# Prompt latent attention of a two-layer trunk: heads taken in pairs, both heads of a query block behind each other

## The chip, the cores and the metric

The kernel runs on one core of one Trainium2 chip. The metric is the device time of one execution in microseconds (us). TensorE is called PE, VectorE DVE, ScalarE ACT, SyncE SP and GpSimd POOL. All matrix products of the stage that changes are in 32-bit floats; each of them shows in the trace as two matmul records.

## What is computed

Two layers of a hybrid decoder trunk run over 1,024 prompt tokens and 8 x 4 sample tokens. The even layer has multi-head latent attention (8 heads), a linear recurrence and memory attention; the odd layer has an mLSTM, a chunk MLP and memory attention. The change lies in the prompt's latent attention of the even layer:

```
def _mla_scores(q_lat, q_rope, lat, krope):
    s = jnp.einsum('bhqc,bkc->bhqk', q_lat, lat) + jnp.einsum('bhqr,bkr->bhqk', q_rope, krope)
    return s.astype(jnp.float32) * MLA_SCALE
...
    def one_block(args):
        ql, qr, i = args
        s = _mla_scores(ql, qr, latent, k_rope)
        qpos = i * ATTN_BLOCK + jnp.arange(ATTN_BLOCK)
        s = jnp.where(kpos[None, :] <= qpos[:, None], s, -jnp.inf)
        p = jax.nn.softmax(s, axis=-1).astype(latent.dtype)
        return jnp.einsum('bhqk,bkc->bhqc', p, latent)
```

A head's query and key have 64 columns of their own (`NOPE`) and 32 rotated ones (`ROPE`); the key's rotated part is one for all heads. A value has 64 columns. Both kernels project the latent to keys and values of each head first, and so work with 96-row queries and keys.

## The kernel before

The engines run their own programs and wait on semaphores; nothing is scheduled by a tool, so the order in the code is the order on each engine.

**Stages around the change.** The even layer's input projection ends near 290 us of the trace. Then come the memory's keys and values, the convolution and the recurrence (LRU) on DVE and ACT up to 392 us. Its buffers `lru_r`, `lru_i`, `lru_t` lie where attention keeps `kT`, `vh`, `wh`, `probs`, so SP loads the heads' weights `wh` only after `lru_done` (L1960).

**Pieces.** A head is prepared in seven pieces (`piece(h, j)`, L2347 to L2360; evacuated by ACT at L2121 to L2129): two for the key (64 rows x 512), three for the query (96 rows x 352), one for the value of all 8 key blocks, one small one for the sample tokens (`w_ukT`). All pieces use PSUM bank 7, so each waits for the evacuation of the one before (`prep_ev`). DVE then rotates the query's 32 rope rows (`rope(h, step)`, L2270 to L2278). Heads 0 and 1 are prepared ahead of attention (14 pieces); heads 2 to 7 inside it, one piece in each unit (`prep_at`, called as `between(n)`).

**Units.** A unit is one head and one block of 128 queries: `UNITS` has 8 heads x 8 blocks, in a head in the order 7, 0, 6, 1, 5, 2, 4, 3, so a block with 1,024 keys is followed by one with 128, and so on. In one turn n of the loop

- PE does the scores of unit n+1 (L803, bank pair 0/1 or 2/3), the piece, the transposes of unit n (L815, banks 4 and 5) and the output of unit n-1 (L827, bank 6, 64 of the 128 partitions);
- DVE normalises unit n (L882, L884), takes mask and maxima of unit n+1 (L874 to L876), multiplies the output of n-1 into `mx` (L891), and does a rope step;
- ACT evacuates the piece, then the transposed probabilities of unit n (L857), then takes the exponentials of unit n+1 (L846).

`probs`, `probsT` and the score banks have two buffers each. After the last unit come memory attention with the sample group's memory attention between (`pe_blocks`), and the sample group's latent attention.

## Time and profile before

| | |
|---|---|
| median of 3 runs | 1883.89 us (1882.79 to 1888.71) |
| the profiled execution | 1891.48 us, its span 1889.8 us |
| PE busy / weight loads busy | 1618.9 us (86%) / 1380.4 us (73%) |
| DVE / ACT busy | 861.1 us (46%) / 537.1 us (28%) |
| granted TensorE clock, mean | 0.916 of full |
| attention stage (first scores to last output) | 436.2 to 727.0 us |

Times of rows are counted from the start of the span. The granted clock of a stretch is 1.00 at full rate (2.4 GHz) and 0.50 at the lower one (1.2 GHz); a number between is a stretch with both. A busy time in a window counts overlapping records once.

### The profile page before, as it was taken

What the parts mean: (1) busy time and instruction counts of PE and PEld (TensorE: products, weight loads), DVE (VectorE), ACT (ScalarE), POOL (GpSimd) and SP (SyncE); (2) the same over time, 40 slices, a digit from 0 to 9 for tenths busy, and PEclk for the clock granted to TensorE, in tenths of its full rate; (3) what the DMA queues carried; (4) which work ended last, traced back from release to release, by engine and by line L of the source; (5) the groups of instructions that cost most, each with busy time, mean ns of one, the idle gap of its engine ahead of it and who ended that gap; (6) DMA issues with size and microseconds to landing.
All of it is one profiled execution on the core that took longest, in us unless ns stands there. A gap on an engine that the chain in (4) does not pass through costs nothing.

```text
span 1889.8 us, 24206 instructions
## 1 busy us (share of the span) xinstructions
PE 1618.9 (86%) x9962; PEld 1380.4 (73%) x9962; DVE 861.1 (46%) x1525; ACT 537.1 (28%) x993; POOL 33.7 (2%) x61
## 2 busy tenths in 40 slices
PE   6999894358999986698998899989999957886994
PEld 6999892225666654455998899987999935874993
DVE  3222625554655565455486322272222224546574
ACT  2003210603333334344254311110002134322343
POOL 1000000000000000000000100000000010000000
PEclk9999997679999998899998899996999987975997
DMA  4111103010100013254552311110111041003561
GB/s 153 53 49 45 34 12 123 26 33 7 57 1 1 1 45 101 62 156 125 181 172 90 143 46 45 45 34 24 45 45 46 12 168 46 1 6 116 174 204 69
DMA packets 51263, 132.12 MB, mean 70 GB/s; under 512 B 6841, under 2 KB 30570, under 8 KB 49938
## 3 DMA queue, kind: packets, MB, share of 16 engines
q1 hardware_dynamic: 46914, 113.12, 18.8%
q0 software_dynamic: 4240, 17.45, 2.5%
q8 instruction: 80, 1.31, 0.3%
q14 instruction: 29, 0.24, 0.0%
HBM read 117.08 MB, written 13.47 MB: 69 GB/s over the span
## 4 chain that ended last, share of the span: by engine, by line
PE 45%; DVE 7%; issue 3%; ACT 2%; DMA 1%; POOL 0%; DVEq 0%; SPq 0%; ACTq 0%; POOLq 0%
PE ps L499 7%; PE ps L500 7%; PE ps L501 7%; PE ps L558 4%; PE ps L560 3%; PE ps L559 3%; PE ps L1269 1%; PE ps L1044 1%; PE ps L1684 1%; PE ps L1898 1%; PE ps L1294 1%; PE ps L949 1%; PE ps L936 1%; PE ps L1550 1%; PE ps L1552 1%
## 5 line engine op out<-in xcount | busy, mean ns | idle before, releaser
L499 PE MATMUL ps<-x_hi,w_hi 128*128 128x352 f32 x1416 | 463.6, 327 | 30.6 <-DVE w_lo L458 28.2
L500 PE MATMUL ps<-x_lo,w_hi 128*128 128x352 f32 x1416 | 459.1, 324 | 0.0
L501 PE MATMUL ps<-x_hi,w_lo 128*128 128x352 f32 x1416 | 458.7, 324 | 0.0
L499 PEld LDWEIGHTS ps<-x_hi,w_hi 128*128 128x128 f32 x1416 | 270.1, 191 | 32.1 <-DVE w_lo L458 29.0
L500 PEld LDWEIGHTS ps<-x_lo,w_hi 128*128 128x128 f32 x1416 | 270.4, 191 | 0.3
L501 PEld LDWEIGHTS ps<-x_hi,w_lo 128*128 128x128 f32 x1416 | 269.7, 190 | 0.0
L452 ACT ACTIVATE w_hi<-w_raw 128x1024 fp32r<-128x1024 f32 (+1 forms) x107 | 123.1, 1152 | 441.3 <-PE ps L501 322.3
L558 PE MATMUL ps<-mx_hi,w_hi 128*128 128x352 f32 x480 | 159.0, 331 | 14.8 <-issue 13.4
L458 DVE TENSOR_TENSOR w_lo<-w_raw,w_hi 128x1024 fp32r<-128x1024 f32 (+1 forms) x107 | 144.1, 1347 | 60.0 <-ACT w_hi L452 59.5
L560 PE MATMUL ps<-mx_hi,w_lo 128*128 128x352 f32 x480 | 155.4, 324 | 0.0
L559 PE MATMUL ps<-mx_lo,w_hi 128*128 128x352 f32 x480 | 155.2, 323 | 0.0
L479 DVE COPY z<-ps 128x352 f32<-128x352 f32 x90 | 46.8, 524 | 219.5 <-PE ps L501 219.5
L558 PEld LDWEIGHTS ps<-mx_hi,w_hi 128*128 128x128 f32 x480 | 91.2, 190 | 16.4 <-issue 13.4
L481 DVE TENSOR_TENSOR mx<-sig,ps 128x352 f32<-128x352 f32 x60 | 30.9, 520 | 155.8 <-ACT sig L467 155.8
L467 ACT ACTIVATE sig<-ps 128x352 f32<-128x352 f32 x72 | 33.3, 465 | 225.3 <-PE ps L501 225.3
L559 PEld LDWEIGHTS ps<-mx_lo,w_hi 128*128 128x128 f32 x480 | 91.6, 191 | 0.8
L560 PEld LDWEIGHTS ps<-mx_hi,w_lo 128*128 128x128 f32 x480 | 91.2, 190 | 0.0
L803 PE MATMUL ps<-kT,qT 96*128 96x512 f32 (+2 forms) x192 | 82.6, 542 | 0.0
L827 PE MATMUL ps<-probsT,vh 128*64 128x128 f32 x576 | 78.3, 282 | 0.5 <-DVE mx L891 0.5
L2347 PE MATMUL ps<-z,wh 128*64 128x512 f32 x64 | 35.5, 683 | 48.0 <-DMA wh<-in_w_mla 46.2
L827 PEld LDWEIGHTS ps<-probsT,vh 128*64 128x64 f32 x576 | 62.5, 139 | 11.6 <-issue 10.5
L815 PEld LDWEIGHTS ps<-ident,probs 128*128 128x128 f32 x288 | 33.4, 144 | 46.7 <-DVE probs L884 36.0
(413 smaller groups left out, 2033.9 us busy)
## 6 DMA issues: line engine op xcount, KB each, us to landing
w_raw<-in_w_out SPq DMA_DIRECT2D x48, 640.0 KB, 3.9
w_raw<-in_w_in SPq DMA_DIRECT2D x59, 512.0 KB, 3.6
page<-in_cache_mla SPq DMA_DIRECT2D x128, 144.0 KB, 2.7
kvs<-in_mem_cache SPq DMA_DIRECT2D x16, 512.0 KB, 9.2
x_res<-in_xT SPq DMA_DIRECT2D x24, 176.0 KB, 2.3
x<-x_next POOLq DMA_DIRECT2D x1, 4224.0 KB, 13.8
x_res<-x SPq DMA_DIRECT2D x24, 176.0 KB, 2.4
out_y<-res POOLq DMA_DIRECT2D x3, 1408.0 KB, 5.9
```

The costliest lines, as they stand in the source:

```text
L452: act.activation(w_hi[:, u % 2, 0:n], w_raw[:, u % 2, 0:n], ACT.Copy).then_inc(w_hi_ready, 1)
L458: dve.tensor_tensor(w_lo[:, u % 2, 0:n], w_raw[:, u % 2, 0:n], w_hi[:, u % 2, 0:n], ALU.subtract).then_inc(w_split, 1)
L479: ins = dve.tensor_copy(out, zz[0:8] if tile.one else zz)
L499: pe.matmul(out, w_hi[:, u % 2, kk], x_hi[:, k, chunk(c)], start=(k == 0), stop=False)
L500: pe.matmul(out, w_hi[:, u % 2, kk], x_lo[:, k, chunk(c)], start=False, stop=False)
L501: mm = pe.matmul(out, w_lo[:, u % 2, kk], x_hi[:, k, chunk(c)], start=False, stop=(k == KX - 1))
L558: pe.matmul(out, w_hi[:, u % 2, kk], mx_hi[:, k, chunk(c)], start=(k == 0), stop=False)
L559: pe.matmul(out, w_hi[:, u % 2, kk], mx_lo[:, k, chunk(c)], start=False, stop=False)
L560: mm = pe.matmul(out, w_lo[:, u % 2, kk], mx_hi[:, k, chunk(c)], start=False, stop=(k == KM - 1))
L803: mm = pe.matmul(s[:, a:b], q_of(u), k_of(u, a, b), start=True, stop=True)
L827: mm = pe.matmul(ps[r:r + 64, 6, 0:P], v_of(u, kt), probsT[:, n % 2, kt, :], start=(kt == 0), stop=(kt == nk - 1))
L2347: mm = pe.matmul(ps[0:64, 7, :], wh[:, s, 288 + 64 * k:352 + 64 * k], z[:, Z_KV + k, 512 * j:512 * j + 512], start=(k == 0), stop=(k == 1))
```

## The change

Heads are handled in pairs. One piece makes the 64 query (or key, or value) columns of two heads at once, 128 columns wide; the 32 rope columns of four heads are one piece of their own (`wr`, `rq`). There are now 42 pieces (9 for each of four pairs, 2 x 3 for the rope) where there were 56. The odd head of a pair keeps its 64 columns in partitions 64 to 127 and the rope rows in 0 to 31, with 32 zero rows between (128 rows); the even head stays as it was (96 rows). The first 12 pieces use eight banks in turn. Six of them stand ahead of the wait on `lru_done` on ACT; their weights lie in the free weight buffer `w_raw` and are loaded before `lru_done`. The other 30 run inside attention, at units 0 to 11, 18 to 26 and 34 to 42.

Units are ordered by pair, block, head: both heads of block 7, both of block 0, both of 6, both of 1 and so on. The output of the two heads is one loop that alternates between the upper and the lower 64 partitions of bank 6, followed by one multiplication over 128 partitions. `probsT` has four buffers.

```diff
...
-        ALTERNATE = [q for a in range(NT // 2) for q in (NT - 1 - a, a)]
-        UNITS = [Unit(h, q, (q + 1) * P) for h in range(H) for q in ALTERNATE]
+        UNITS = [Unit(2 * p + r, q, (q + 1) * P, 8 * p + 2 * a + w)
+                 for p in range(H // 2) for a in range(NT // 2) for w, q in enumerate((NT - 1 - a, a))
+                 for r in range(2)]
+        Pair = namedtuple("Pair", "p q nk first second")
+        PAIRS = [Pair(u.h // 2, u.q, u.nk // P, n, n + 1) for n, u in enumerate(UNITS) if n % 2 == 0]
...
+        def pair_at(n):
+
+            return n // 2 - 1 if n % 2 == 0 and n else None
...
+        ROPE_PIECE = (0, 21)
+        PAIR_PIECE = (3, 12, 24, 33)
+        N_FIRST, N_PIECES = 12, 42
...
+        def piece_bank(i):
+            return i % 8 if i < N_FIRST else 7
...
+            def output(m):
+                w = PAIRS[m]
+                pe.wait_ge(pt_ev, FILLS[w.second][1])
+                pe.wait_ge(prep_ev, PAIR_PIECE[w.p] + 7)
+                if m:
+                    pe.wait_ge(o_done, m)
+                for kt in range(w.nk):
+                    for r, n in enumerate((w.first, w.second)):
+                        mm = pe.matmul(ps[64 * r:64 * r + 64, 6, 0:P],
+                                       vh[:, w.p % 2, kt, 64 * r:64 * r + 64], probsT[:, n % 4, kt, :],
+                                       start=(kt == 0), stop=(kt == w.nk - 1), skip_group_check=True)
                 mm.then_inc(o_ready, 1)
...
+                if pair_at(n) is not None:
+                    output(pair_at(n))
+            output(len(PAIRS) - 1)
...
         def prep_at(n):
-            if n >= 64 or n // 8 + 2 >= H or n % 8 >= PIECES:
-                return None
-            return n // 8 + 2, n % 8
+
+            if n < 12:
+                return N_FIRST + n
+            if 18 <= n < 27:
+                return PAIR_PIECE[2] + n - 18
+            if 34 <= n < 43:
+                return PAIR_PIECE[3] + n - 34
+            return None
...
+            sp.wait_ge(w_split, 24)
+            sp.dma_start(wr[:, :, :], x["w_qr"]).then_inc(wr_in, 16)
+            for p in range(2):
+                sp.dma_start(wh[:, p, :], x["w_mla"][p]).then_inc(wh_in[p], 16)
+            sp.dma_start(table[:, :], x["page_table"]).then_inc(tbl_in, 16)
             sp.wait_ge(lru_done, 4)
-            for h in range(H):
-                if h >= 4:
-                    sp.wait_ge(prep_z, PIECES * (h - 3))
-                sp.dma_start(wh[:, h % 4, :], x["w_mla"][h]).then_inc(wh_in[h % 4], 16)
...
+            for i in range(6):
+                evacuate_piece(i)
             act.wait_ge(lru_done, 4)
-            for h in range(2):
-                for j in range(PIECES):
-                    evacuate_piece(h, j)
-            act_attention(act, lambda n: prep_at(n) and evacuate_piece(*prep_at(n)))
+            for i in range(6, N_FIRST):
+                evacuate_piece(i)
+            act_attention(act, lambda n: prep_at(n) and evacuate_piece(prep_at(n)))
...
+            v.mark(dve.memset(qT[32:64, 1:4:2, :], 0.0))
+            v.mark(dve.memset(kT[32:64, 1:4:2, :], 0.0))
             for s in range(4):
-                v.mark(dve.tensor_copy(kT[64:QD, s, :], raw[:, 0:T]))
+                r = 64 * (1 - s % 2)
+                v.mark(dve.tensor_copy(kT[r:r + ROPE, s, :], raw[:, 0:T]))
...
+            for step in range(3):
+                rope(0, step)
             for h in range(2):
-                for step in range(4):
-                    rope(h, step)
+                rope_sum(h)
...
+            pe.wait_ge(lru_sig, 24)
+            for i in range(6):
+                piece(i)
+            pe.wait_ge(mem_ev, 5)
+            for i in range(6, N_FIRST):
+                piece(i)
```

**DVE between the recurrence and the first maxima, before.** A row names the line, the operation, what it writes and reads, and the semaphores it waits on. After the key's rope (L2257 to L2262) each of the two heads has a rope of its own, and each waits for that head's query pieces (`prep_ev`).

```order
L2260 TENSOR_TENSOR z<-rope_a,rope_b 32x1056 [waits v_step]
L2262 COPY kT<-z 32x1024 [waits v_step]
L2262 COPY kT<-z 32x1024 x3
L2264 COPY stat<-eps 128x1 [waits v_step]
L2270 STREAM_SHUFFLE rope_a<-qT 32x1056 [waits prep_ev]
L2272 TENSOR_TENSOR rope_b<-qT,rope_tab 32x1056
L2274 TENSOR_TENSOR rope_a<-rope_a,rope_tab 32x1056 [waits v_step]
L2276 TENSOR_TENSOR qT<-rope_a,rope_b 32x1056 [waits v_step]
L2278 COPY qsr<-qT 32x8x4 [waits rope_ready]
L2270 STREAM_SHUFFLE rope_a<-qT 32x1056 [waits prep_ev,v_step]
```

The same place in the changed kernel, up to the first mask (L905), which is next:

```order
L2305 TENSOR_TENSOR z<-rope_a,rope_b 32x1056 [waits v_step]
L2306 MEMSET qT 32x2x1056 [waits v_step]
L2307 MEMSET kT 32x2x1024
L2310 COPY kT<-z 32x1024 x4
L2312 COPY stat<-eps 128x1 [waits v_step]
L2318 STREAM_SHUFFLE rope_a<-rq 128x1056 [waits prep_ev]
L2320 TENSOR_TENSOR rope_b<-rq,rope_tab 128x1056
L2322 TENSOR_TENSOR rope_a<-rope_a,rope_tab 128x1056 [waits v_step]
L2327 TENSOR_TENSOR qT<-rope_a,rope_b 32x1056 [waits v_step]
L2329 COPY qsr<-qT 32x8x4 [waits rope_ready]
L2327 TENSOR_TENSOR qT<-rope_a,rope_b 32x1056 [waits v_step]
L2329 COPY qsr<-qT 32x8x4 [waits rope_ready]
```

Two memsets are new. The shuffle and the two products are done once, for four heads, and wait only for the three rope pieces; a sum for each head follows.

**PE between the recurrence and the first scores, before** (key pieces and two of three query pieces of the first head; the rest of the 14 pieces goes on in the same way, each with a wait for `prep_ev`):

```order
L2336 MATMUL ps<-z,lru_w 128x352 [waits lru_sig] x18
L2347 MATMUL ps<-z,wh 64x512 [waits wh_in0,lat_ready,branch_in]
L2347 MATMUL ps<-z,wh 64x512
L2347 MATMUL ps<-z,wh 64x512 [waits prep_ev]
L2347 MATMUL ps<-z,wh 64x512
L2351 MATMUL ps<-z,wh 96x352 [waits prep_ev]
L2351 MATMUL ps<-z,wh 96x352 x2
L2351 MATMUL ps<-z,wh 96x352 [waits prep_ev]
L2351 MATMUL ps<-z,wh 96x352 x2
```

The changed kernel there, both heads together, up to the last value piece:

```order
L2392 MATMUL ps<-z,lru_w 128x352 [waits lru_sig] x18
L2408 MATMUL ps<-z,wr 128x352 [waits lru_sig,wr_in,lat_ready,branch_in]
L2408 MATMUL ps<-z,wr 128x352 x8
L2412 MATMUL ps<-z,wh 128x352 [waits wh_in0]
L2412 MATMUL ps<-z,wh 128x352 x8
L2416 MATMUL ps<-z,wh 128x512 [waits mem_ev]
L2416 MATMUL ps<-z,wh 128x512 x3
L2421 MATMUL ps<-wh,z 128x128 [waits prep_ev]
L2421 MATMUL ps<-wh,z 128x128 x7
L2421 MATMUL ps<-wh,z 128x128 [waits prep_ev]
L2421 MATMUL ps<-wh,z 128x128 x7
```

The waits for an evacuation between one query piece and the next are gone, and the first wait is for `wr_in`, not for weights that are loaded after `lru_done`.

**PE inside attention, one and a half turns, before** (a block of 128 keys, then one of 896):

```order
L815 MATMUL ps<-ident,probs 128x128 [waits pt_ev,pn_ready]
L827 MATMUL ps<-probsT,vh 64x128 [waits pt_ev]
L827 MATMUL ps<-probsT,vh 64x128 x7
L803 MATMUL ps<-kT,qT 128x256 [waits prep_ev,rope_ready,p_ready]
L2351 MATMUL ps<-z,wh 96x352 [waits prep_ev]
L2351 MATMUL ps<-z,wh 96x352 x2
L815 MATMUL ps<-ident,probs 128x128 [waits pt_ev,pn_ready]
```

The changed kernel at the first short unit: after its transpose come the 16 products of the pair's output (8 key blocks x 2 heads), and only then the scores of the next long block.

```order
L845 MATMUL ps<-ident,probs 128x128 [waits pt_ev,pn_ready]
L857 MATMUL ps<-probsT,vh 64x128 [waits prep_ev,pt_ev]
L857 MATMUL ps<-probsT,vh 64x128 x15
L833 MATMUL ps<-kT,qT 128x512 [waits prep_ev,rope_ready,p_ready]
L833 MATMUL ps<-kT,qT 128x384
L2416 MATMUL ps<-z,wh 128x512 [waits prep_ev]
L2416 MATMUL ps<-z,wh 128x512
L845 MATMUL ps<-ident,probs 128x128 [waits pt_ev,pn_ready]
L833 MATMUL ps<-kT,qT 128x512 [waits prep_ev,rope_ready,p_ready]
```

The output moved from every turn to every second one, and stands between the short unit's transpose and the scores of the next long block.

## Rows read from the trace of the kernel before

**Rows 1.** Windows: the whole stage, a head with pieces, one without, and memory attention

```profile
core 0: us, PE busy (x) PEld busy (x) DVE busy (x) ACT busy (x) POOL busy (x), PEclk, DMA share, GB/s
436.20:727.00 290.80, 270.56 (x1431) 175.65 (x1430) 167.08 (x421) 110.86 (x268) 0.00 (x0) 0.98 0.05 18
553.40:591.20 37.80, 36.29 (x197) 23.49 (x194) 22.36 (x54) 14.31 (x35) 0.00 (x0) 1.00 0.00 1
667.70:697.10 29.40, 25.49 (x136) 16.48 (x134) 19.71 (x52) 11.71 (x29) 0.00 (x0) 0.94 0.01 4
760.00:800.00 40.00, 27.34 (x243) 21.13 (x243) 16.64 (x41) 14.35 (x41) 0.00 (x0) 0.79 0.24 73
```

**Rows 2.** Timeline from the recurrence's end to the first scores: start, us, engine, line

```profile
392.33 44.33 SPq L1960 DMA_DIRECT2D wh<-in_w_mla  x6
392.34 1.30 DVE L2257 STREAM_SHUFFLE rope_a<-z 32x1056 f32<-32x1056 f32 x1
...
395.17 3.65 PE L2347 MATMUL ps<-z,wh 128*64 128x512 f32 x4 [46.17 <-DMA wh<-in_w_mla]
...
397.38 2.49 DVE L2262 COPY kT<-z 32x1024 f32<-32x1024 f32 x4
...
404.73 2.02 PE L2351 MATMUL ps<-z,wh 128*96 128x352 f32 x6 [0.55 <-ACT qT L2123]
...
436.23 3.90 PE L803 MATMUL ps<-kT,qT 96*128 96x512 f32 x6
```

**Rows 3.** DMA issues from 365 to 380 us: KB, us to landing

```profile
rope_tab<-in_rope_tab SPq DMA_DIRECT2D x1, 1056.0 KB, 4.9
```

**Rows 4.** Timeline at 369 us: when that load is issued

```profile
369.43 0.33 SPq L1955 DMA_DIRECT2D rope_tab<-in_rope_tab  x1
```

**Rows 5.** Groups by line and form on DVE: busy us, mean ns of one

```profile
L1759 DVE MEMSET m_c<- 128x1024 f32 x1 | 0.9, 912 | 0.2 <-issue 0.2
```

**Rows 6.** Groups on PE, 436 to 727 us: products, then weight loads of the output

```profile
L827 PE MATMUL ps<-probsT,vh 128*64 128x128 f32 x576 | 78.3, 282 | 0.5 <-DVE mx L891 0.5
L2351 PE MATMUL ps<-z,wh 128*96 128x352 f32 x108 | 34.9, 459 | 0.0
L2347 PE MATMUL ps<-z,wh 128*64 128x512 f32 x48 | 23.2, 605 | 0.0
L2356 PE MATMUL ps<-wh,z 128*128 128x64 f32 x192 | 22.1, 273 | 0.0
L2360 PE MATMUL ps<-qT,w_ukT 64*128 64x32 f32 x27 | 4.3, 277 | 0.0
```

**Rows 7.** Timeline on PE in memory attention: one row's products, two heads' products

```profile
1577.11 1.09 PE L936 MATMUL ps<-ident,probs 128*128 128x128 f32 x8 [0.81 <-DVE probs L1010]
1578.13 1.09 PE L949 MATMUL ps<-probsT,vm 128*64 128x128 f32 x16
```

**Rows 8.** Timeline in the stage: a long unit's output, full clock and a low stretch

```profile
670.39 1.09 PE L815 MATMUL ps<-ident,probs 128*128 128x128 f32 x8 [2.12 <-DVE probs L884]
...
672.85 2.99 PE L803 MATMUL ps<-kT,qT 96*128 96x512 f32 x4
...
675.88 1.96 PE L827 MATMUL ps<-probsT,vh 128*64 128x128 f32 x16
...
680.88 1.56 PE L803 MATMUL ps<-kT,qT 96*128 96x512 f32 x4
```

**Rows 9.** Groups by form on DVE and ACT in the stage

```profile
L882 DVE RECIPROCAL stat<-stat 128x1 f32<-128x1 f32 x64 | 10.4, 162 | 13.8 <-ACT probs L846 12.8
L875 DVE TENSOR_REDUCE stat<-ps 128x1 f32<-128x896 f32 x8 | 8.7, 1091 | 0.3
L884 DVE TENSOR_SCALAR probs<-probs,stat 128x1024 f32<-128x1024 f32 x8 | 6.0, 753 | 0.3
L884 DVE TENSOR_SCALAR probs<-probs,stat 128x128 f32<-128x128 f32 x8 | 2.3, 287 | 0.3
...
L857 ACT ACTIVATE probsT<-ps 128x512 f32<-128x512 f32 x48 | 27.9, 596 | 44.1 <-PE ps L815 44.1
L846 ACT ACTIVATION_READ_ACCUMULATOR probs<-ps,stat 128x1 f32 x64 | 13.2, 206 | 0.0
L846 ACT ACTIVATE probs<-ps,stat 128x1024 f32<-128x1024 f32 x8 | 8.9, 1115 | 7.5 <-DVE stat L876 7.5
L846 ACT ACTIVATE probs<-ps,stat 128x896 f32<-128x896 f32 x8 | 8.0, 998 | 2.5 <-DVE stat L876 2.5
```

225 lines of the change are left out of this document (124 added, 101 removed).

## The prediction

> **What bounds the kernel now.** The page and the windows come first. The attention stage lasts 290.8 us at a mean clock of 0.98, and PE is busy 270.6 us of it [rows 1]. That looks like a stage bound by PE, but two windows of one head each say more: a head with pieces takes 37.8 us with PE busy 36.3, a head without pieces 29.4 us with PE busy 25.5 [rows 1]. So pieces cost 8.4 us a head. The groups of PE give the work in them: 34.9 + 23.2 + 22.1 + 4.3 = 84.5 us for six heads, 14.1 us a head [rows 6]. So 60% of the piece work lies on the path; the rest fills waits, as the 2.12 us before a long unit's transposes [rows 8]. Without pieces the turn is bound by a chain around three engines (exponentials, normalise, transposes, evacuation, exponentials), not by PE.
>
> Ahead of the stage, the timeline shows the recurrence's end at 392.3 us and the first scores at 436.2: 43.9 us. PE has waited 46.17 us for `wh` at its start, then does 14 pieces in single file, each query piece 2.02 us and then a wait of 0.55 for ACT [rows 2].
>
> **The start.** All 12 pieces' products can run before `lru_done`. The rope table is issued at 369.43 [rows 4], and its 1,056 KB land in 4.9 us [rows 3], some 216 KB a us. `wr` (384 KB) and two `wh` (448 KB each) queue behind it: at that pace `wr` lands near 376, the last `wh` near 380.5. PE then has six pieces of the rope and query kind at 1.94 us (34.9 / 18), two of keys at 1.93 (23.2 / 12) [rows 6], two of values (16 records of 128 columns each, as the output that took 1.96 us [rows 8], so 2 x 2.0) and two small ones at 0.7: 21 us at full clock. PE has idled, so it starts at the lower clock; the first key piece before took 3.65 us as well [rows 2]. I add 4 us: PE is ready near 401.
>
> DVE then sets the start. The key's rope runs from 392.34 to 397.4. Two memsets are new: 2,112 and 2,048 elements a partition; the nearest row has 912 ns for 1,024 [rows 5], so 1.8 us each, 3.6 together (not below 2 us if only the fixed part counted twice, not over 4). The four copies take 2.49 [rows 2]: 403.5. Shuffle and two products for four heads at 1.3 us each (the shuffle over 32 partitions has 1.30 [rows 2]; that 128 partitions cost the same is my choice, since the other ropes' elements a partition are the same): 407.4, and the first head's sum 1.25: scores start at 408.7. Against 436.2 that is **27.5 us earlier**. ACT's six evacuations after `lru_done` (some 4 us) are hidden under DVE. Bounds: 23 us if PE stays at the lower clock a few us longer or the shuffle grows with partitions, 30 if both memsets cost a microsecond.
>
> **The pair's output.** The trace has the same form in memory attention: 16 records for two heads, alternating between 64 columns of the array each, take 1.09 us, and 8 transposes, 128 columns wide, take 1.09 too [rows 7]. A single head's 16 records take 1.96 [rows 8]. So two heads together should cost what one does: 78.3 us of output [rows 6] becomes 39, and a long pair takes 1.96 us.
> The Trainium skill says otherwise for weights (TensorE: Matmul & The Clock Gate, Part 3, The mechanism): a weight load overlaps running products only when the row groups differ, and here they are the same. By it each of 576 loads would stand beside its product. The trace disagrees: 139 ns is a load's mean duration on this line, while 16 records with their loads lie within 1.96 us, 0.12 each.
>
> **The turn without pieces.** I walk the first round of four units (1,024, 1,024, 128, 128, next 896 keys), with 0.15 us for hand-overs in each leg. Long to long: reciprocal 0.16, normalise 0.75, transposes 1.09, second evacuation 0.60, exponentials 1.11 + 0.21 = 3.92 + 0.15 = 4.1 us [rows 8, 9]. Long to short: the same with an exponential of about 0.37: 3.3. Then short, short, long. Here the new order bites: PE has the transpose, the pair's output and only then the long scores. Normalise 0.16 + 0.29, transpose 0.28, output 1.96, scores of 896 keys 1.8 (1.56 for 768 [rows 8]), mask 0.30, maxima 1.09, sign 0.15, exponentials 1.00 + 0.21 = 7.24, with hand-overs 7.4 [rows 9]. The round takes 14.8 us. The rounds of 7, 6 and 5 blocks give, by the same legs, 13.8, 13.0 and 13.9 (the last ends on 1,024 keys). A pair of heads: **55.4 us**, 27.7 a head. The same walk over the order of before gives 27.7 a head too, against 29.4 measured at a clock of 0.94 [rows 1]. So for bare units the change gives nothing: what the paired output saves is lost where a long block follows a long one and where the output stands ahead of long scores.
>
> **The pieces in the stage.** Three pairs, each 3 x 1.94 + 2 x 1.93 + 4.0 + 1.4 = 15.1 us, and three rope pieces, 5.8: 51 us where 84.5 stood. They also meet more idle time on PE: per pair of heads 2 x 25.5 - 9.8 (78.3 / 8) = 41 us of PE in 55.4, so 14 us idle. Bounds for what stays on the path: 0 (all in gaps) and 60% as before, 31 us. A piece right behind the short units' scores lies on the leg of 7.4 us, those of the long legs mostly do not; one piece in two in the first rounds, fewer in the others, and DVE's rope steps (1.25 each) twice: I take **16 us**.
>
> **The sum.** Stage: 4 x 55.4 = 221.6, first and last unit's edges 4, pieces 16: 241.6 at full clock. Clock: the head without pieces ran at 0.94 and took 29.4 instead of the walk's 27.7, 6%; half of the new stage is as thin, so 8 us. Stage 249.6, against 290.8: 41 us less. With the start 27.5 less, and a low clock in the first scores of either kernel (3.90 us for 1,152 keys [rows 2]): -68.5. What follows is unchanged and moves as a block. Span 1889.8 - 68.5 = 1821; this execution was 7.6 us above the median of the runs shown, so the median goes from 1883.9 to **1816**.
> Own range: start 23 to 30; stage 234 to 264 by the pieces' bounds, so 27 to 57 less; 1797 to 1834.
>
> **Rivals.**
> *The packing does not hold* (5%): two heads' output costs twice one's. For: they now alternate for 16 to 32 records, and `probsT` has more buffers. Against: rows 7. Then the leg of 7.4 us grows by 1.96 in the first round and 1.7, 1.5, 1.2 in the others, some 6.4 a pair of heads: +26 us, 1842.
> *Loads beside products* (1%): each weight load of the output stands alone, 576 x 0.139 = 80 us more on PE; with 40 of idle taken up, about +50: 1866. This is what the Trainium skill's rule above would do.
> *The pieces are hidden completely* (10%): the stage loses 16 us more: 1800.
> *The start is late* (7%): `wr` waits for a late `lru_m`, or PE stays at the lower clock for all 12 pieces (2 x 21 us from 376: 418 instead of 409): +10, 1826.
> *Slower than before, by the clock* (3%). PE idles in every long leg, and memory attention, where it is busy 27.3 of 40 us, ran at 0.79 [rows 1]. At the lower clock 896 keys took 2.99 us against 1.8. The gain of 68 us is gone when 136 us of PE's streaming are done at half rate, of a stage of 318 us: 241.6 us at full clock spread over 318 is a mean granted clock of 0.76, with no wait to absorb it. At 0.70 the stage would take 345 us and the kernel 1911. Against it: the thin heads of before stayed at 0.94.
> *No change* (1%): only if start and stage fail together.
> My forecast has the remaining 73%. A measurement of this kernel tells 0.3% (5.6 us) from no change. Faster: 96%; the same: 1%; slower: 3%. The range of 8 in 10 leaves out the packing and clock rivals: 1799 to 1837.
>
> **What the changed profile would show.** First scores near 409 us, PE at pieces from 376 on, and DVE, not PE, as their releaser. An output of 32 records in about 2 us for a long pair. The stage's end near 658 us, heads 56 us a pair in the last pair (no pieces) and 60 to 62 in those with pieces. PE's clock in the stage 0.92 to 0.95. I would be wrong most easily in the share of pieces on the path and in the clock.

## The result, and the profile after

The changed kernel takes 1815.3 us (median of 4 runs, 1808.04 to 1820.12), the kernel before 1885.6 beside it (4 runs, 1882.79 to 1888.71). The ratio is 0.9624, with a 95% interval of 0.9586 to 0.9661: faster by 70.3 us. A repeat in another set of runs gave 1814.44 us and 0.9618 (0.9597 to 0.9639). The forecast was 1816.

First the page of the changed kernel, its first part: busy us, share of the span and instructions.

```profile
PE 1529.0 (85%) x9766; PEld 1328.0 (74%) x9766; DVE 830.7 (46%) x1471; ACT 541.0 (30%) x999; POOL 33.5 (2%) x61
```

PE has 89.9 us less to do than before (1618.9), more than the 83.5 us by which the profiled executions differ (spans 1889.8 and 1806.3). The windows say where the time came from. Columns as in [rows 1]; the first row is the whole stage, the second the second pair of heads, with nine pieces in its turns, the third the last pair, which has none, the fourth all that follows the stage.

```profile
core 0: us, PE busy (x) PEld busy (x) DVE busy (x) ACT busy (x) POOL busy (x), PEclk, DMA share, GB/s
406.60:647.10 240.50, 198.58 (x1274) 129.35 (x1274) 137.57 (x370) 111.87 (x269) 0.00 (x0) 0.96 0.03 12
471.90:529.70 57.80, 49.85 (x332) 32.69 (x330) 33.93 (x92) 29.20 (x71) 0.00 (x0) 1.00 0.00 1
587.50:647.10 59.60, 40.36 (x275) 26.60 (x274) 29.42 (x85) 22.91 (x56) 0.00 (x0) 0.89 0.00 1
647.10:1806.30 1159.20, 1011.88 (x6712) 906.45 (x6712) 520.07 (x860) 330.14 (x596) 23.89 (x42) 0.91 0.28 88
```

The stage took 290.8 us with PE busy 270.6 [rows 1]; it takes 240.5 with PE busy 198.6. PE lost 72 us of work and the stage 50.3: PE now idles 42 us in it where it idled 20, so PE's work alone no longer sets its length. The last pair, 59.6 us at a clock of 0.89, is no shorter than two bare heads of before (2 x 29.4 at 0.94 [rows 1]). All of the stage's gain lies in the heads that have pieces: 57.8 us for the second pair, and as much for the third, instead of 2 x 37.8.

The 83.5 us between the two profiled executions are made up of 3.4 ahead of the recurrence's end, 26.3 at the start, 50.3 in the stage and 3.6 behind it. The first is no effect of an edit that any run isolates: in the other variants of the changed kernel the recurrence ended at 388.4 to 391.3 us, in the kernel before and its two variants at 391.7 to 393.0.

The start, in the timeline from 360 to 425 us (start, us, engine, line):

```profile
366.42 0.43 SPq L1991 DMA_DIRECT2D wr<-in_w_qr  x1
...
372.06 8.01 PE L2408 MATMUL ps<-z,wr 128*128 128x352 f32 x18 [26.45 <-DMA wr<-in_w_qr]
...
379.91 5.49 PE L2412 MATMUL ps<-z,wh 128*128 128x352 f32 x18
...
388.67 3.73 PE L2421 MATMUL ps<-wh,z 128*128 128x128 f32 x32
...
388.98 1.37 DVE L2302 STREAM_SHUFFLE rope_a<-z 32x1056 f32<-32x1056 f32 x1
...
394.53 1.82 DVE L2306 MEMSET qT<- 32x2112 f32 x1 [0.49 <-DVE z L2305]
...
396.73 1.76 DVE L2307 MEMSET kT<- 32x2048 f32 x1 [0.38 <-issue]
...
398.52 2.83 DVE L2310 COPY kT<-z 32x1024 f32<-32x1024 f32 x4
...
401.46 1.32 DVE L2318 STREAM_SHUFFLE rope_a<-rq 128x1056 f32<-128x1056 f32 x1
...
405.24 1.25 DVE L2327 TENSOR_TENSOR qT<-rope_a,rope_b 32x1056 f32<-32x1056 f32 x1
...
406.60 5.92 PE L833 MATMUL ps<-kT,qT 96*128 96x512 f32 x8 [13.62 <-DVE qT L2327]
```

PE starts its pieces at 372.1, is slower in the first three of them (8.01 us for 18 records, 5.49 for the next 18), and is through near 393. The releaser of the first scores is DVE's sum, 13.62 us later. From the recurrence's end (the shuffle, 388.98) to the first scores it is 17.6 us, where it was 43.9 [rows 2].

The products of the stage by group (line, shapes, count | busy us, mean ns of one record | idle time before them and its releaser):

```profile
L845 PE MATMUL ps<-ident,probs 128*128 128x128 f32 x288 | 44.7, 282 | 41.2 <-DVE probs L915 41.2
L857 PE MATMUL ps<-probsT,vh 128*64 128x128 f32 x576 | 41.7, 294 | 0.7 <-ACT probsT L888 0.7
...
L2412 PE MATMUL ps<-z,wh 128*128 128x352 f32 x54 | 17.5, 459 | 0.0
L2421 PE MATMUL ps<-wh,z 128*128 128x128 f32 x96 | 11.7, 275 | 0.0
L2416 PE MATMUL ps<-z,wh 128*128 128x512 f32 x24 | 11.3, 592 | 0.0
...
L2408 PE MATMUL ps<-z,wr 128*128 128x352 f32 x18 | 5.8, 459 | 0.0
...
L2428 PE MATMUL ps<-qT,w_ukT 64*128 64x32 f32 x24 | 3.8, 278 | 0.0
```

The output's 576 records are busy 41.7 us instead of 78.3 [rows 6], at nearly the same mean for one (294 and 282 ns): two records run beside each other. The piece work in the stage is 17.5 + 11.7 + 11.3 + 5.8 + 3.8 = 50.1 us instead of 84.5. Nearly all idle time of PE is now in front of the transposes, 41.2 us, released by DVE's normalise.

A round's turning point, the timeline from 479 to 490.5 us, rows of PE, DVE and ACT:

```profile
479.92 0.21 ACT L877 ACTIVATION_READ_ACCUMULATOR probs<-ps,stat 128x1 f32 x1
...
480.94 0.27 PE L845 MATMUL ps<-ident,probs 128*128 128x128 f32 x1
...
481.14 1.97 PE L857 MATMUL ps<-probsT,vh 128*64 128x128 f32 x32
...
483.04 1.77 PE L833 MATMUL ps<-kT,qT 96*128 96x512 f32 x4
...
483.47 1.25 DVE L2327 TENSOR_TENSOR qT<-rope_a,rope_b 32x1056 f32<-32x1056 f32 x1
...
484.65 1.94 PE L2412 MATMUL ps<-z,wh 128*128 128x352 f32 x6
...
485.69 1.09 DVE L906 TENSOR_REDUCE stat<-ps 128x1 f32<-128x896 f32 x1
...
486.62 0.46 ACT L2165 ACTIVATE qT<-ps 64x352 f32<-64x352 f32 x1 [3.90 <-PE ps L2412]
...
487.09 0.46 ACT L2166 ACTIVATE qT<-ps 64x352 f32<-64x352 f32 x1
...
487.57 0.28 ACT L888 ACTIVATE probsT<-ps 128x128 f32<-128x128 f32 x1
...
487.75 1.00 ACT L877 ACTIVATE probs<-ps,stat 128x896 f32<-128x896 f32 x1
...
488.64 0.20 ACT L877 ACTIVATION_READ_ACCUMULATOR probs<-ps,stat 128x1 f32 x1
```

32 records of output take 1.97 us, the time of one head's 16 before (1.96, [rows 8]). The leg from the end of a short unit's exponentials (480.1) over its transpose, the output, the long scores and the maxima to the end of the long exponentials (488.8) is the one that the walk gave 7.4 us. Here, with a piece and a rope sum in it, it is 8.7: the scores end at 484.8, but DVE is in the rope's sum until 484.7 and in the second short unit's normalise after it, and takes the maxima only at 485.69. They and the sign are done at 487.0, but ACT has to evacuate the piece first, which PE ends at 486.6 (the two rows at 486.62 and 487.09), and then the transpose (487.57): the exponentials start 0.8 us late, at 487.75.

### The profile page after: what moved, and what is told of

Its sections match the earlier page's. It is cut to its first block, busy times and chain, and to the rows that moved or that the text cites. A ratio compares the mean times of both kernels' runs of the same rounds, so it can differ in the third digit from the quotient of the medians.

```text
span 1806.3 us, 23728 instructions
## 1 busy us (share of the span) xinstructions
PE 1529.0 (85%) x9766; PEld 1328.0 (74%) x9766; DVE 830.7 (46%) x1471; ACT 541.0 (30%) x999; POOL 33.5 (2%) x61
## 3 DMA queue, kind: packets, MB, share of 16 engines
q1 hardware_dynamic: 46546, 113.12, 19.6%
## 4 chain that ended last, share of the span: by engine, by line
PE 47%; DVE 7%; issue 3%; ACT 2%; DMA 1%; POOL 0%; DVEq 0%; SPq 0%; ACTq 0%; POOLq 0%
PE ps L504 8%; PE ps L505 7%; PE ps L506 7%; PE ps L563 4%; PE ps L565 4%; PE ps L564 4%; PE ps L1303 1%; PE ps L1078 1%; PE ps L1718 1%; PE ps L1932 1%; PE ps L1328 1%; PE ps L978 1%; PE ps L965 1%; PE ps L1584 1%; PE ps L1586 1%
## 5 line engine op out<-in xcount | busy, mean ns | idle before, releaser
L833 PE MATMUL ps<-kT,qT 96*128 96x512 f32 (+4 forms) x192 | 79.8, 528 | 13.6 <-DVE qT L2327 13.6
L845 PEld LDWEIGHTS ps<-ident,probs 128*128 128x128 f32 x288 | 31.8, 141 | 65.9 <-DVE probs L915 63.2
L845 PE MATMUL ps<-ident,probs 128*128 128x128 f32 x288 | 44.7, 282 | 41.2 <-DVE probs L915 41.2
L888 ACT ACTIVATE probsT<-ps 128x512 f32<-128x512 f32 (+3 forms) x96 | 43.6, 488 | 72.6 <-PE ps L845 72.1
L965 PE MATMUL ps<-ident,probs 128*128 128x128 f32 x128 | 25.4, 363 | 46.8 <-DVE probs L1039 46.8
```

Of the source, the lines that this page charges most:

```text
L833: mm = pe.matmul(s[:, a:b], q_of(u), k_of(u, a, b), start=True, stop=True)
L845: mm = pe.transpose(ps[:, 4 + f % 2, (kt - k0) * P:(kt - k0 + 1) * P], pr[:, kt * P:(kt + 1) * P], ident[:, :])
L888: act.activation(flat(probsT[:, n % 4, k0:k1, :]), ps[:, 4 + f % 2, 0:(k1 - k0) * P], ACT.Copy).then_inc(pt_ev, 1)
```

## The experiments

The table has, for every kernel, the stage in its profiled execution (first scores, end of the last output, length, mean granted clock), the median and the ratio to the kernel before in the same set of runs. Each edit is against the changed kernel, except where another is named.

| kernel | first scores | end | stage us | clock | median us | ratio (95%) |
|---|---|---|---|---|---|---|
| before | 436.2 | 727.0 | 290.8 | 0.98 | 1885.6 | |
| changed | 406.6 | 647.1 | 240.5 | 0.96 | 1815.3 | 0.9624 (0.9586 to 0.9661) |
| changed, again | 408.9 | 648.6 | 239.7 | 0.96 | 1814.4 | 0.9618 (0.9597 to 0.9639) |
| e1 alternate | 408.1 | 651.8 | 243.7 | 0.95 | 1818.4 | 0.9625 (0.9601 to 0.9649) |
| e2 output apart | 408.4 | 664.6 | 256.2 | 0.96 | 1829.8 | 0.9681 (0.9654 to 0.9708) |
| e3 late load | 415.2 | 654.1 | 238.9 | 0.97 | 1817.9 | 0.9628 (0.9598 to 0.9658) |
| e4 one bank | 407.9 | 646.2 | 238.3 | 0.96 | 1816.2 | 0.9616 (0.9592 to 0.9641) |
| e5 no pieces | 405.9 | 647.5 | 241.6 | 0.86 | 1811.6 | 0.9618 (0.9579 to 0.9657) |
| e6 short DVE row | 402.8 | 643.7 | 240.9 | 0.96 | 1809.8 | 0.9601 (0.9558 to 0.9644) |
| e7 order alone | 435.4 | 726.2 | 290.8 | 0.98 | 1890.1 | 1.0029 (1.0012 to 1.0045) |
| e8 pieces twice | 407.1 | 686.3 | 279.2 | 0.96 | 1856.4 | 0.9851 (0.9808 to 0.9894) |
| e9 order and output | 435.5 | 700.6 | 265.1 | 0.94 | 1871.0 | 0.9919 (0.9894 to 0.9943) |
| e10 short row, filler | 401.6 | 641.2 | 239.6 | 0.99 | 1809.8 | 0.9599 (0.9575 to 0.9623) |
| e11 no pieces, filler | 407.8 | 636.4 | 228.6 | 0.99 | 1801.8 | 0.9561 (0.9536 to 0.9586) |

A mean clock of c is a stretch with 2(1 - c) of it at the lower level: 0.96 in 240.5 us is 19 us, 0.86 in 241.6 is 68 us, 0.99 in 228.6 is 5. The clock is given to a hundredth, so each of these is good to some 2 us.

### The order of the units

**e1.** The turns of a pair alternate between a long and a short block again; the output of both heads stays together.

```
-                 for p in range(H // 2) for a in range(NT // 2) for w, q in enumerate((NT - 1 - a, a))
-                 for r in range(2)]
+                 for p in range(H // 2) for a in range(NT // 2) for r in range(2)
+                 for w, q in enumerate((NT - 1 - a, a))]
...
-        PAIRS = [Pair(u.h // 2, u.q, u.nk // P, n, n + 1) for n, u in enumerate(UNITS) if n % 2 == 0]
+        PAIRS = [Pair(u.h // 2, u.q, u.nk // P, n, n + 2) for n, u in enumerate(UNITS) if n % 4 < 2]
...
-            return n // 2 - 1 if n % 2 == 0 and n else None
+            return 2 * (n // 4) if n % 4 == 3 else 2 * (n // 4) - 1 if n % 4 == 0 and n else None
```

> The changed kernel with one thing undone: in a round the units go long, short, long, short again (head 1 of the pair after head 0), while the two heads' outputs are still made together, each once both are evacuated. Theory A (the walk of the prediction: the chain around three engines and the leg behind the short units both count, and they even out): the stage stays within 3 us of the changed kernel's 240.5 us, the ratio to the kernel before within 0.003 of 0.9624. Rival B (a long block behind a long one exposes its whole chain, and this is the main loss): alternating saves 8 us or more, stage 232 us or less. Rival C (the gain comes from the new order itself): the stage grows by 10 us or more.

The stage is 243.7 us at 0.95, 3.2 us longer than the changed kernel's and 0.2 beyond what was expected; the ratio, 0.9625, can't be told from 0.9624. So alternating neither saves 8 us nor costs 10.

**e7.** Only the order, on the kernel before: pairs, block, head; each unit keeps its own output, and the pieces of before stand in 14 of 16 turns.

```
-        UNITS = [Unit(h, q, (q + 1) * P) for h in range(H) for q in ALTERNATE]
+        UNITS = [Unit(2 * p + r, q, (q + 1) * P) for p in range(H // 2) for q in ALTERNATE for r in range(2)]
...
-            if n >= 64 or n // 8 + 2 >= H or n % 8 >= PIECES:
+            if n >= 48 or n % 16 >= 2 * PIECES:
                 return None
-            return n // 8 + 2, n % 8
+            return 2 + 2 * (n // 16) + n % 16 // PIECES, n % 16 % PIECES
```

> The kernel before with the new order of units alone: both heads of a pair behind each other on each block, the pieces of two heads in 14 of 16 turns and the rope steps moved with them; pieces per head, one output per head and the start stay as they were. Theory A (order alone gives nothing, since a long block behind a long one exposes the chain): stage 290.8 + 2 = 293 us, ratio 1.00 within 0.004. Rival B (the order is the gain): stage 15 us shorter or more. Rival C (the order costs): 8 us longer or more.

The window of its stage:

```profile
435.40:726.20 290.80, 268.01 (x1431) 174.58 (x1430) 166.17 (x421) 110.77 (x268) 0.00 (x0) 0.98 0.05 18
```

This is the stage of before to the tenth of a microsecond. The ratio, 1.0029, puts the whole kernel 0.1 to 0.5% slower, and the traces don't show where: the execution of before that was profiled (span 1889.8) lay 6 us above the median of its own runs, so its span is no measure for this one's 1890.2. The order by itself brings no gain: it only makes room for what follows.

### The output of two heads together

**e2.** The two loops of the output are exchanged, so that one head's 16 records follow the other's.

```
-                for kt in range(w.nk):
-                    for r, n in enumerate((w.first, w.second)):
+                for r, n in enumerate((w.first, w.second)):
+                    for kt in range(w.nk):
```

> The changed kernel with the output's two loops exchanged: first all products of one head, then all of the other, so that they no longer alternate between the two halves of the array; the count of instructions is the same. Theory A (alternating heads share the array's time, and the output stands on the leg from a short unit to the next long scores): a long pair's 32 records take 3.7 to 3.9 us instead of 2.0, and the stage grows by 26 us (6.4 a pair of heads), ratio 0.976. Rival B (the output is off the path, hidden under DVE and ACT): stage within 5 us. Rival C (records of both heads overlap even in this order): output records as in the changed kernel, no change.

The stage's window, and the output of a long pair in the timeline of PE:

```profile
408.40:664.60 256.20, 218.63 (x1274) 149.45 (x1275) 137.57 (x371) 112.27 (x269) 0.00 (x0) 0.96 0.03 11
```

```profile
487.48 3.33 PE L857 MATMUL ps<-probsT,vh 128*64 128x128 f32 x32
```

3.33 us instead of 1.97 for the same 32 records with the same operands: only the order of the records differs. So the time of one head for two is real, and comes from the alternation between the two halves of the columns. Its worth against this order is 15.7 us of stage and 11 us of time (0.0057 of 1886; each ratio has an interval of 0.003 to 0.004 to either side), not the 26 at which I had priced its failure. PE has 20 us more to do (218.6 against 198.6), and a fifth of that still finds idle time. The products of the output are busy 61.3 us here, 41.7 in the changed kernel and 78.3 in the kernel before [rows 6], so this edit takes back little more than half of what the paired output saves.

The Trainium skill (TensorE: Matmul & The Clock Gate, Part 3, The mechanism) has a weight load overlap running products only where the row groups differ; another sentence of the same section also names loads into the background weight buffer. The first rule by itself doesn't hold here. The rows of the array are the same for all these loads, and loads and products overlap even without the second head: 16 records of one head, with loads of 139 ns each, take 1.96 us [rows 8], less than the loads alone end to end (2.2 us). So different column halves aren't needed for that. What alternating adds is that products of the two halves run beside each other, 32 records in 1.97 us. No run shows by which way the loads get in. The row of the loads, from the groups of the kernel before, 436 to 727 us:

```profile
L827 PEld LDWEIGHTS ps<-probsT,vh 128*64 128x64 f32 x576 | 62.5, 139 | 11.6 <-issue 10.5 <-ACT probsT L857 0.3
```

**e9.** e7 with the paired output: one loop for both heads, `probsT` with four buffers, `wh` in the space of `w_raw`; the pieces, the ropes and the start remain those of before.

```
-                    mm = pe.matmul(ps[r:r + 64, 6, 0:P], v_of(u, kt),
-                                   probsT[:, n % 2, kt, :], start=(kt == 0), stop=(kt == nk - 1))
+                    for r in range(2):
+                        mm = pe.matmul(ps[64 * r:64 * r + 64, 6, 0:P], v_of(UNITS[2 * m + r], kt),
+                                       probsT[:, (2 * m + r) % 4, kt, :], start=(kt == 0), stop=(kt == nk - 1),
+                                       skip_group_check=True)
...
-                if n:
-                    output(n - 1)
+                if n % 2 == 0 and n:
+                    output(n // 2 - 1)
```

> The kernel before with the new order of units and, on top, the two heads' output made together (alternating halves of the array, one multiplication over 128 partitions, four buffers of transposed probabilities); pieces per head and the start stay as before. Theory A (the output is worth what undoing it cost, 15.7 us, and the rest of the stage's 50 us comes from fewer and shorter pieces and ropes): stage 273 to 278 us, ratio 0.993. Rival B (the output is worth more while PE is loaded with long pieces, and carries most of the gain): stage 262 or less. Rival C (off the path): 287 or more.

The window of its stage:

```profile
435.50:700.60 265.10, 235.10 (x1431) 149.18 (x1430) 156.22 (x389) 109.97 (x268) 0.00 (x0) 0.94 0.06 20
```

25.7 us less than e7, for 33 us less PE work; 273 to 278 us were expected, so this was missed, between the two answers. The expectation took the 15.7 us of e2 for the worth of the paired output. But e9 saves 35.0 us of output products (busy 79.6 us in e7, 44.6 here) and e2 adds only 19.6. Per microsecond of PE work the two agree: 25.7 / 32.9 and 15.7 / 20.0 are both 0.78. So the difference is no sign that the saving is worth less beside the new pieces. The new pieces and ropes, on top of the paired output, are worth what is left: 265.1 - 240.5 = 24.6 us of stage, for 36.5 us less PE work. No run has them without it.

The gain of e9 lies in the pairs with pieces alone. From the first transposes of a pair to those of the next it takes 65.3, 65.7 and 66.8 us, where e7 takes 75.5, 77.6 and 74.6. In the last pair, which has no pieces, the same stretch up to the last transposes is 57.4 us where it is 53.8 in e7: PE has less to do there, and its clock is 0.82 instead of 0.95.

### The pieces, and the clock

**e8.** The products of every piece inside the stage are issued twice, the second time over the first.

```
+                for again in range(2 if i >= N_FIRST else 1):
+                    mm = products(what, p, j, b, s)
+                mm.then_inc(prep_z, 1)
```

> The changed kernel with each of the 30 pieces inside attention computed twice into the same bank, which adds some 50 us of PE work and nothing on other engines. Theory A (PE's waits absorb about two thirds of the first 50 us, and little is left for a second): plus 30 to 37 us, stage 271 to 278, ratio 0.981. Rival B (PE has waits to spare everywhere): plus 16 us or less. Rival C (every microsecond of piece work counts): plus 50.

The window of its stage:

```profile
407.10:686.30 279.20, 243.87 (x1490) 163.07 (x1490) 137.75 (x370) 112.04 (x269) 0.00 (x0) 0.96 0.03 10
```

45.3 us more of PE (243.87 - 198.58) lengthen the stage by 38.7 (30 to 37 expected): 0.85 us for each. What is added right behind the pieces finds hardly a gap any more.

**e5.** No pieces inside the stage: all heads use the queries, keys and values of heads 0 and 1.

```
-            return qT[rows_of_head(u.h), u.h % 4, u.q * P:u.q * P + P]
+            return qT[rows_of_head(u.h), u.h % 2, u.q * P:u.q * P + P]
...
-            if n < 12:
-                return N_FIRST + n
-            if 18 <= n < 27:
-                return PAIR_PIECE[2] + n - 18
-            if 34 <= n < 43:
-                return PAIR_PIECE[3] + n - 34
             return None
```

> Leaves out part of the computation: all eight heads use the queries, keys and values of heads 0 and 1, so the 30 pieces inside attention, their evacuations and the ropes of heads 2 to 7 are gone; everything else is as in the changed kernel. Theory A (the prediction's sum): the pieces have 16 us of the stage on the path, of about 50 us of PE work; stage 240.5 - 16 = 224 us, ratio 0.954. Rival B (as before the change, 60% of their work is on the path): minus 30 us, stage 210, ratio 0.947. Rival C (already hidden): within 4 us.

The window of its stage:

```profile
405.90:647.50 241.60, 173.94 (x1058) 112.39 (x1058) 126.78 (x360) 92.27 (x224) 0.00 (x0) 0.86 0.03 9
```

All piece work of the stage, its evacuations and its rope steps are gone, and the stage, expected at 224 us, is 1 us longer. Taken alone this would say that the pieces are hidden completely. But the clock fell from 0.96 to 0.86, and the timeline of PE shows records at the lower level: the output of a long pair takes 3.21 us where it took 1.97.

```profile
541.02 3.21 PE L856 MATMUL ps<-probsT,vh 128*64 128x128 f32 x32
...
549.69 1.09 PE L845 MATMUL ps<-ident,probs 128*128 128x128 f32 x7 [2.14 <-DVE probs L914]
```

**e11.** e5, and PE does two products that nobody reads, into the pieces' bank, ahead of the transposes of each long unit, where it waited.

```
+            def filler(n):
+                pe.wait_ge(prep_ev, N_FIRST)
+                for a in range(2):
+                    pe.matmul(bank(7), ident[:, :], z[:, Z_KV + a, 0:512], start=True, stop=True)
...
+                if n % 4 < 2 and prep_at(n) is None:
+                    filler(n)
```

> Leaves out the same part of the computation as the run without pieces (all heads use the data of heads 0 and 1), and adds products that nobody reads: 1.7 us of PE work in each turn of a long unit (32 turns, 54 us in all), where PE waits for the normalised probabilities. Theory A (without pieces the low clock gave back what the pieces had cost: 69 of 241.6 us at the lower level): the clock stays up, low time under 20 us, and the stage gets shorter by doing more: 228 to 234 us. Rival B (the stage was bound by the chain alone and the clock is harmless): no change, 240 to 243. Rival C (the extra work is on the path): 246 or more.

The window of its stage, and the same place in the timeline of PE:

```profile
407.80:636.40 228.60, 201.51 (x1186) 117.42 (x1186) 126.60 (x360) 92.41 (x224) 0.00 (x0) 0.99 0.03 10
```

```profile
539.37 1.88 PE L864 MATMUL ps<-z,ident 128*128 128x512 f32 x4
541.67 0.98 PE L845 MATMUL ps<-ident,probs 128*128 128x128 f32 x7 [0.42 <-DVE probs L921]
```

The filler is 128 records in 32 turns, at 1.88 us a turn 60 us of PE, and the stage is 13.0 us shorter for it. The wait for DVE shrinks from 2.14 to 0.42 us, since the filler lies in it. Nothing but the filler differs between the two, and the products that both have are busy 173.9 us in e5 and some 141 in e11 (201.5 - 60.2). What took the gain of e5 away was the clock.

The difference to the changed kernel, 240.5 - 228.6 = 11.9 us, is not yet the price of the pieces. The last pair has pieces in neither kernel, and yet 4.1 us of it lie there, from that pair's first scores to the stage's end (changed kernel first, then e11):

```profile
583.67:647.10 63.43, 44.19 (x288) 28.43 (x286) 31.94 (x91) 23.67 (x59) 0.00 (x0) 0.89 0.00 1
577.05:636.40 59.35, 51.51 (x320) 30.48 (x318) 31.95 (x91) 23.84 (x59) 0.00 (x0) 1.00 0.00 1
```

The starts of the transposes of one unit after the other (L845 in the timelines of PE) separate the effects, since a turn of one kind at one clock repeats within 0.1 us, from the second pair to the third and from run to run. From the first transposes of a pair of heads to those of the next it takes:

| | us |
|---|---|
| changed kernel, first pair, 12 pieces in its turns | 59.6 |
| changed kernel, second and third pair, 9 pieces each | 57.8 |
| e11, no pieces, filler | 55.7 to 55.9 |
| no pieces, no filler, full clock: added up from such turns of e5 and e11 | 54.2 |

So the 30 pieces, with their evacuations and rope steps, cost 5.4 + 3.6 + 3.6 = 12.6 us. The filler is not free: it costs 1.6 us a pair, most of it in the second long turn of the rounds of 5 and 6 blocks, 6.4 us in all. And the clock cost e5 13.0 + 6.4 = 19.4 us against full clock, for some 68 us at the lower level: 0.3 us for each. In the changed kernel it cost 5.7 us, in two turns of the last pair, 6.56 us instead of 3.76 and 6.33 instead of 3.44. The parts add up: four bare pairs and the edges 222.2, pieces 12.6, clock 5.7, together 240.5 us.

The first 50 us of piece work cost 12.6 us, the next 45 (e8) cost 38.7.

### The start

**e3.** `wr` and `wh` are loaded after `lru_done`, as `wh` was before.

```
             sp.wait_ge(w_split, 24)
+            sp.wait_ge(lru_done, 4)
             sp.dma_start(wr[:, :, :], x["w_qr"]).then_inc(wr_in, 16)
...
-            sp.wait_ge(lru_done, 4)
```

> The changed kernel with the three loads of the heads' weights put behind the recurrence's end on SP's queue, as before the change. Theory A (the start is set by DVE's 17.6 us behind the recurrence as long as PE's 12 pieces are done by then; loaded late they are not): wr lands about 3 us after the recurrence's end, PE needs 21 us at full clock plus 4 at the lower one, then two small evacuations: first scores 28 to 30 us after the recurrence's end instead of 17.6, so 11 us more, ratio 0.968. Rival B (the fewer and paired pieces are what shortens the start, and the early load is of no use): within 3 us of the changed kernel. Rival C (the early load is the whole gain): first scores 40 us or more after the recurrence's end, plus 23 us.

PE's timeline, first piece to first scores:

```profile
394.69 7.08 PE L2408 MATMUL ps<-z,wr 128*128 128x352 f32 x18 [47.05 <-DMA wr<-in_w_qr]
...
414.03 0.64 PE L2428 MATMUL ps<-qT,w_ukT 64*128 64x32 f32 x8
415.18 3.67 PE L833 MATMUL ps<-kT,qT 96*128 96x512 f32 x8 [0.51 <-ACT qs L2172]
```

PE starts 22.6 us later and is on the path now (the first scores wait for ACT's evacuation of the last piece), yet they come only 6.6 us later relative to the recurrence's end (24.2 against 17.6, and 28 to 30 expected). And they run at full clock: 3.67 us for 8 records, which took 5.92. The stage is 238.9 us. From the recurrence's end to the stage's end it is 263.1 us, where the changed kernel and its repeat have 258.1 and 257.3: by the traces the early load is worth 5 to 6 us. The ratio, 0.9628, can't be told from 0.9624; with intervals of 0.003 to either side the runs neither show these microseconds nor rule them out.

**e4.** All pieces in bank 7, each waiting for the evacuation of the one before.

```
         def piece_bank(i):
-            return i % 8 if i < N_FIRST else 7
+            return 7
...
-                if i >= N_FIRST:
+                if i:
                     pe.wait_ge(prep_ev, i)
...
+            pe.wait_ge(mem_ev, 5)
             for i in range(6):
                 piece(i)
-            pe.wait_ge(mem_ev, 5)
```

> The changed kernel with the first 12 pieces all in PSUM bank 7, each waiting for the evacuation of the one before, as before the change; loads stay early. Theory A (hidden): pieces 0 to 5 are done before the recurrence's end; the six others take 1.93 + 1.3 us (two of keys), 1.95 + 0.7 (two of values) and about 1 (two small), some 14 us, against DVE's 17.6: first scores at the same distance from the recurrence's end, ratio unchanged within 0.002. Rival B (the banks matter): first scores 5 us or more later.

PE's timeline, last piece and first scores:

```profile
406.82 0.63 PE L2426 MATMUL ps<-qT,w_ukT 64*128 64x32 f32 x4 [0.31 <-ACT qs L2172]
407.85 2.42 PE L833 MATMUL ps<-kT,qT 96*128 96x512 f32 x4 [0.41 <-ACT qs L2172]
```

The wait for `mem_ev` now stands ahead of all pieces, which delays nothing: PE starts them 17.0 us before the recurrence's end, 16.9 in the changed kernel. The pieces in single file last until 407.5 and the first scores stand at 407.85, 17.8 us after the recurrence's end: about the same as with eight banks, with nothing to spare. The sixth piece ends at 392.8, 2.7 us behind the recurrence's end, and not before it as expected; the wait on the path at the end is ACT's evacuation of the last one.

**e6.** The DVE row is cut: both memsets go to POOL, and the key copies of the second pair's slots go into turns 4 and 5.

```
+            gp.memset(kT[32:64, 1:4:2, :], 0.0).then_inc(zero_done, 1)
+            gp.memset(qT[32:64, 1:4:2, :], 0.0).then_inc(zero_done, 1)
...
-            v.mark(dve.memset(qT[32:64, 1:4:2, :], 0.0))
-            v.mark(dve.memset(kT[32:64, 1:4:2, :], 0.0))
-            for s in range(4):
+            for s in range(2):
...
+                elif n in (4, 5):
+                    s, r = n - 2, 64 * (1 - n % 2)
+                    dve.tensor_copy(kT[r:r + ROPE, s, :], raw[:, 0:T]).then_inc(k_more, 1)
```

> The changed kernel with two things taken off DVE between the recurrence and the first scores: both memsets go to POOL right after the recurrence, and the key's rope rows for heads 2 and 3 are copied inside attention (units 4 and 5). Theory A (DVE's row of operations sets the first scores): memsets with the waits around them 4.4 us, two copies 1.4: first scores 11.9 us behind the recurrence's end instead of 17.6, ratio 0.9595. Rival B (POOL's memsets are slow or share DVE's port): POOL takes over 8 us for them and the first odd scores wait for it, no gain. Rival C (PE's pieces are the true bound): gain under 1 us.

The timeline from the recurrence's end to the first scores:

```profile
390.90 1.80 POOL L2066 MEMSET kT<- 32x2048 f32 x1 [69.20 <-DVE stat L2301]
...
392.64 1.85 POOL L2067 MEMSET qT<- 32x2112 f32 x1
...
402.77 6.20 PE L837 MATMUL ps<-kT,qT 96*128 96x512 f32 x8 [8.65 <-DVE qT L2331]
```

First scores 11.9 us after the recurrence's end instead of 17.6, the stage unchanged (240.9): what leaves the row of DVE leaves the time of the trace. PE also waits for POOL's memsets ahead of the first scores, but they are through at 394.5. The median is 5 us under that of the changed kernel; the intervals of the two ratios overlap.

**e10.** e6 with the filler of e11 in the 16 long turns that have no piece.

```
+            def filler(n):
+                pe.wait_ge(prep_ev, 24 if n < 18 else 33 if n < 34 else N_PIECES)
+                for a in range(2):
+                    pe.matmul(bank(7), ident[:, :], z[:, Z_KV + a, 0:512], start=True, stop=True)
```

> The kernel with the short DVE row ahead of the first scores, and the same unread products in the long units' turns that have no piece (16 turns). Theory A: the stage's low time of 18 to 25 us falls below 10, stage 241.0 to 236-238, first scores at 11.9 us behind the recurrence's end; ratio 0.958. Rival B (at these turns PE has no room): stage 243 or more.

The clock rises to 0.99, and the stage is 239.6 us against e6's 240.9 (236 to 238 expected). Two effects nearly cancel: the last pair is 4.3 us shorter (51 us from its first to its last transposes instead of 55), and the three pairs before it, where the clock was nearly full already, are together 2.9 us longer by the filler's own price. Here the filler about pays for itself. e6 and e10 have the same median, 1809.8; they are the fastest versions found that do the whole computation, 0.3% under the changed kernel by the medians, but the intervals of the ratios overlap.

### The changed kernel again

> The changed kernel again, beside the others on one chip. Every theory: ratio 0.962 within 0.003, stage 238 to 244 us, recurrence's end 388 to 391 us.

All came out so but the recurrence's end, which stands at 391.3. It shows how much of the time is not the change's. The windows of memory attention right behind the stage, the changed kernel and its repeat:

```profile
647.10:712.90 65.80, 39.86 (x327) 29.25 (x328) 29.63 (x69) 26.81 (x86) 0.00 (x0) 0.82 0.40 117
```

```profile
648.60:718.80 70.20, 44.27 (x328) 32.29 (x328) 29.61 (x69) 26.81 (x86) 0.00 (x0) 0.73 0.37 109
```

The same instructions take 4.4 us longer at 0.73 than at 0.82, and all that follows the stage takes 1168.3 us instead of 1159.2.

## Why the prediction was right, step by step

**The start**, forecast at 27.5 us less: 26.3. The parts fit: the memsets took 1.82 and 1.76 us (1.8 each), the shuffle over 128 partitions 1.32 (1.3), the sum 1.25. PE started at 372 (forecast 376; 3.4 us of this are the earlier end of the recurrence). PE was through at 393, not 401, and as that is hidden it changed nothing; in e4 it is through only at 407.5, with the scores in the same place. What was left out: 0.49 and 0.38 us of wait at the memsets and 2.83 instead of 2.49 for the copies. That DVE's row sets the start is shown from both sides: e4 (PE's work longer, 17.8 us instead of 17.6) and e6 (DVE's row shorter, 5.7 us gained).

**The output of a pair costs what one head's does**: 1.97 us for 32 records, 41.7 us for all. Confirmed by e2. The price of its failure was mis-sized: 26 us forecast, 15.7 in the stage. I had let a second head's output add 1.96 us for a long pair; in e2 it adds 3.33 - 1.97 = 1.36, and 26 x 1.36 / 1.96 is 18, near the 15.7. Those 1.36 us stand in full in the turn behind the output of 8 blocks, 6.84 us instead of 5.48: there the output lies on the path, as the walk had it.

**Bare units gain nothing**: forecast 55.4 us a pair in either order, 225.6 us for four with the edges. Measured at full clock: 54.2 a pair, 222.2 in all. The walk was 3.4 us too long over the stage. That the change brings nothing there is borne out by the times: the last pair takes 59.6 us at a clock of 0.89, two bare heads before took 58.8 at 0.94, and with e9 the last pair gets no shorter than with e7. The reason given for it is only half of it. At full clock e7's bare turns after a long output are longer than those with the paired output (3.75 us against 2.70, 3.23 against 2.83), so the paired output does save something in the chain; what takes it back is the lower clock. e7 has the order without a gain, e1 has its undoing with 3.2 us more in the stage.

**Pieces on the path**, forecast at 16 us: 12.6. The step was right in kind (neither hidden completely nor 60% on the path) and about a quarter too large. e5 alone would have given 0, and wrongly so.

**The clock**, forecast at +8 us and 0.92 to 0.95: 5.7 us and 0.96. Its cost was too large, since half of the new stage was not as thin as the bare head; the second and the third pair ran at 1.00. The three terms, 3.4, 3.4 and 2.3 us too large, are what made the stage 240.5 and not 249.6, 50.3 us less instead of 41. The second and the third pair took 57.8 and not 60 to 62.

**What follows moves as a block**: within the scatter. It took 1162.8 us before, 1159.2 in the profiled execution of the changed kernel and 1168.3 in its repeat. Half of the nine microseconds between the last two lies in memory attention, whose clock varies. The same part is 1160.6 to 1168.2 us in the experiments that leave it as it is.

**Luck.** Start and stage together give 76.6 us by the traces, 8 more than the 68.5 forecast: the stage came out 9.1 us shorter than forecast, the start's gain 1.2 smaller. The spans of the profiled executions differ by 83.5 us, but the medians by 70.3 only. The 13.2 us between the two come from which executions were profiled: the one of the changed kernel is the fastest of its four, 7.3 us under their median, the one of the kernel before lies 5.9 us above the median of its runs. So by the medians the parts outside start and stage gave 6 us back, and no run shows why. That brought the measured 1815.3 to within a microsecond of the forecast 1816; its parts were not that good, and so much of the agreement is luck.

**The rivals.** The packing that doesn't hold and loads beside products: excluded by e2 and by the 1.97 us. Pieces hidden completely: its time (1800) was not reached, and e11 shows that they still cost. The late start: no. Slower by the clock: the mechanism exists, and e5 is its clearest case (0.86, 19 us), but from there to the break-even of 0.76 is far.

## What to carry to other kernels

A stage that looks bound by one engine may have a chain close beneath: take two windows, with and without the side work, before pricing a saving. Here 72 us less of PE work gave 50. An experiment that undoes an edit must put back the same amount of work before its price is taken for the edit's worth: e2 puts back 20 us where the paired output saves 35, and the 15.7 us that it costs are not the 25.7 that the output brings. Products that use half the columns of the array should alternate between the halves: 32 records in 1.97 us, 3.33 in the other order. And an experiment that removes work from PE must be read with its granted clock beside it; if that falls, put work that nobody reads into the waits, and compare again, turn by turn, because that work has a price of its own (6.4 us here).

## What the runs showed of the hardware

- Less work on PE was no faster, and then more work was: 241.6 us with PE busy 173.9 at a clock of 0.86, 228.6 us with PE busy 201.5 at 0.99. I had expected the idle time to cost a little, not to take back all that the removal of 50 us of work gave.
- The first 18 records of pieces after PE had waited took 8.01 us, the next 18 took 5.49, and in e3, where the pieces run right into the scores, the first scores were at full clock (8 records in 3.67 us against 5.92). A late start of work on PE gave back part of its own cost, 1.6 us of the stage.
- A memset of 2,112 elements a partition takes 1.82 us on DVE and 1.85 on POOL, one of 2,048 takes 1.76 and 1.80: POOL, otherwise idle there, does it as fast by the trace, whose spans on POOL are rough.
